# Forget-gate sums written by the matmul into all the partitions that the scores read, in place of eight transfers between partitions

## The reference, cut to what matters

```python
log_f = jax.nn.log_sigmoid(f_logit + b_forget)         # (B, 8 heads, 512)
c = jnp.cumsum(log_f, axis=-1)
logits = einsum('bhqd,bhkd->bhqk', q * Dh**-0.5, k)     # Dh = 64
logits = logits + c[:, :, q, None] - c[:, :, None, k]   # causal mask, softmax, @ v
```

## Time and profile before

| | us |
|---|---|
| median of 3 runs | 1793.53 |
| the runs | 1791.86, 1793.53, 1794.62 |
| the profiled execution | 1794.67 |
| its span | 1792.6 |
| mean granted TensorE clock | 0.996 |
| PE busy | 1767.9 (99% of the span) |
| PEld busy | 1491.5 (83%) |
| DVE busy | 1110.7 (62%) |
| ACT busy | 791.4 (44%) |
| POOL busy | 136.3 (8%) |

### The profile page before, as it was taken

How to read it: one execution, slowest core, us unless ns; L and a number is a source line. 1 busy time by engine, 2 the same in 40 slices (tenths; PEclk the granted TensorE clock), 3 DMA queues, 4 the chain that set the end, 5 groups by cost and what they waited for, 6 DMA issues and landing times.

```text
span 1792.6 us, 23145 instructions
## 1 busy us (share of the span) xinstructions
PE 1767.9 (99%) x8992; PEld 1491.5 (83%) x8992; DVE 1110.7 (62%) x1871; ACT 791.4 (44%) x1419; POOL 136.3 (8%) x133
## 2 busy tenths in 40 slices
PE   9999999999999999999999999999999999999998
PEld 7798788888888888887888888898888888888886
DVE  4578644344345666686764755656879776366375
ACT  6563432222235555544533433456766544144144
POOL 2003200000004100002000000023010110000000
PEclk9999999999999999999999999999999999999999
DMA  5212333333323222122333333322011233333331
GB/s 164 74 48 67 95 95 94 96 104 94 94 95 99 67 66 63 60 69 74 94 105 95 94 95 101 98 77 74 26 54 41 59 95 94 96 104 95 95 119 68
DMA packets 128328, 152.32 MB, mean 85 GB/s; under 512 B 9338, under 2 KB 102044, under 8 KB 128220
## 3 DMA queue, kind: packets, MB, share of 16 engines
q1 hardware_dynamic: 128060, 150.78, 27.4%
q10 hardware_dynamic: 160, 0.07, 0.0%
HBM read 148.59 MB, written 2.10 MB: 84 GB/s over the span
## 4 chain that ended last, share of the span: by engine, by line
PE 93%; DVE 3%; ACT 2%; issue 1%; POOL 1%; DMA 0%; SPq 0%; DVEq 0%; POOLq 0%; ACTq 0%
PE bk L1756 23%; PE bk L1758 22%; PE bk L1757 22%; PE bk L1785 5%; PE bk L1787 5%; PE bk L1786 5%; PE bk L1761 4%; PE bk L1857 2%; PE bk L1823 1%; PE bk L1830 1%; PE bk L1844 1%; DVE XT L1926 1%; PE bk L1846 1%; PE bk L1845 1%; ACT R L2105 0%
## 5 line engine op out<-in xcount | busy, mean ns | idle before, releaser
L1756 PE MATMUL bk<-R,WH 128*128 128x512 f32 x1764 | 691.8, 392 | 5.1 <-DVE R L1920 3.1
L1758 PE MATMUL bk<-R,WL 128*128 128x512 f32 x1764 | 687.4, 390 | 0.0
L1757 PE MATMUL bk<-R,WH 128*128 128x512 f32 x1764 | 687.1, 389 | 0.0
L1914 DVE TENSOR_TENSOR WL<-RAW,WH 128x1024 fp32r<-128x1024 f32 (+4 forms) x278 | 344.9, 1241 | 497.2 <-ACT WH L2101 496.5
L2101 ACT ACTIVATE WH<-RAW 128x1024 fp32r<-128x1024 f32 (+4 forms) x278 | 288.0, 1036 | 593.1 <-PE bk L1758 537.3
L1756 PEld LDWEIGHTS bk<-R,WH 128*128 128x128 f32 x1764 | 331.6, 188 | 73.3 <-issue 6.2
L1758 PEld LDWEIGHTS bk<-R,WL 128*128 128x128 f32 x1764 | 331.5, 188 | 69.6
L1757 PEld LDWEIGHTS bk<-R,WH 128*128 128x128 f32 x1764 | 331.8, 188 | 67.2
L1785 PE MATMUL bk<-WH,R 128*128 128x512 f32 (+4 forms) x528 | 187.4, 355 | 0.0
L1787 PE MATMUL bk<-WL,R 128*128 128x512 f32 (+4 forms) x528 | 179.1, 339 | 0.0
L1786 PE MATMUL bk<-WH,R 128*128 128x512 f32 (+4 forms) x528 | 178.7, 339 | 0.0
(11 more groups left out here) (155 smaller groups left out, 1617.6 us busy)
## 6 DMA issues: line engine op xcount, KB each, us to landing
RAW<-in_ffn_w_up_dram SPq DMA_DIRECT2D x176, 256.0 KB, 3.1
RAW<-in_ffn_w_down_dram SPq DMA_DIRECT2D x44, 512.0 KB, 3.7
RAW<-in_w_gate_dram SPq DMA_DIRECT2D x44, 256.0 KB, 2.8
RAW<-in_w_up_dram SPq DMA_DIRECT2D x44, 256.0 KB, 3.1
RAW<-in_w_down_dram SPq DMA_DIRECT2D x22, 512.0 KB, 3.7
RAW<-in_da_w_qkv_dram SPq DMA_DIRECT2D x32, 256.0 KB, 3.0
RAW<-in_w_out_dram SPq DMA_DIRECT2D x8, 512.0 KB, 3.7
RAW<-in_da_w_qkv_dram SPq DMA_DIRECT2D x8, 512.0 KB, 3.5
```

What stands on the lines that cost most here:

```text
L1756: e.matmul(dst, lh, rh, start=start, stop=False)
L1757: e.matmul(dst, lh, rl, start=False, stop=False)
L1758: return e.matmul(dst, ll, rh, start=False, stop=stop)
L1914: e.tensor_tensor(low, RAW[:, r, 0:m], high.bitcast(F32), ALU.subtract).then_inc(on["wlo_dve"], 1)
```

## The change

`gate_log` now writes the gates' logs not as 8 columns per token tile but as 128: in a slot of `FS` that POOL has zeroed (`gate_zero`), each head's value is repeated 4 times, and the 32 columns again in the second half, so that `gate_sum` has a 128-column stationary operand and writes c to partitions 0 to 31 and 64 to 95, four per head, with zeros in the others. The 8 DMAs, `gate_base` and `gate_cq` are gone. A new step `gate_rows` on DVE, once for the query's and once for the key's operand, is a `tensor_scalar` and a `scalar_tensor_tensor` over 128x512: high x column + (low x column + column), with three columns of 0, 1 and -1 each, so that of a head's four partitions one carries the high part, one the low part, and two a constant. It writes `R[cq]` and `ckf` directly. The planner's costs are changed with it.

```diff
-    "gate_in": {"dve": 2}, "gate_exp": {"act": 2}, "gate_log": {"dve": 1}, "gate_sum": {"pe": 1},
-    "gate_base": {"dve": 1}, "gate_rows": {}, "gate_cq": {"act": 1},
+    "gate_in": {"dve": 2}, "gate_exp": {"act": 2}, "gate_log": {"dve": 2}, "gate_zero": {"pool": 1}, "gate_sum": {"pe": 1},
+    "gate_rows": {"dve": 2},
...
-                "gate_in": 400.0, "gate_log": 190.0, ...
+                "gate_in": 400.0, "gate_log": 560.0, "gate_rows": 1450.0, ...
...
-            st = yield step("gate_log", dst=lf, z=z, e1=e1, after=[st.act])
+            st = yield step("gate_log", dst=FS[:, lx.i, 0:S], z=z, e1=e1, after=[st.act, zero.pool])
...
-            cut = yield from split_pair(c, BK[b.i][0:8, :], [st.pe], rows=slice(0, 8))
+            cut = yield from split_pair(c, BK[b.i][:, :], [st.pe])
...
-            for n, (d, s) in enumerate(((cqf, FG.cqf), (ckf, FG.ckf))):
-                st = yield step("gate_base", dst=d, c=C_BASE + n, after=counts([s.free, x_done[0]]))
-                bases.append(st.dve)
-            emit("gate_rows", rows=[(0, c.h.i, FG.cqf.i), (1, c.l.i, FG.cqf.i), (2, c.h.i, FG.ckf.i), (3, c.l.i, FG.ckf.i)],
-                 after=[cut, *bases])
-            placed = (s_c, 16 + 128)
-            ready_at[id(s_c), 144] = at_time(bases[1]) + 4000.0
...
-            st = yield step("gate_cq", dst=R[:, cq.i, :], src=cqf, after=counts([placed, cq.free]))
-            cq.ready = [st.act]
+            st = yield step("gate_rows", c=C_GATE, t=t, h=R[:, c.h.i, :], l=R[:, c.l.i, :], dst=R[:, cq.i, :],
+                            after=counts([cut, st.pe, cq.free]))
+            cq.ready = [st.dve]
+            st = yield step("gate_rows", c=C_GATE + 3, t=ckf, h=R[:, c.h.i, :], l=R[:, c.l.i, :], dst=ckf, after=counts(FG.ckf.free))
+            placed = st.dve
...
-                        mm = e.matmul(BK[st.bank][0:8, n * P:S], st.lf[:, 8 * n:8 * n + 8], st.tri[:, 0:S - n * P],
+                        mm = e.matmul(BK[st.bank][:, n * P:S], st.lf[:, n * P:n * P + P], st.tri[:, 0:S - n * P],
                                       start=n == 0, stop=n == 3)
...
+                    high, low, other = (CN[:, st.c + n:st.c + n + 1] for n in range(3))
+                    e.tensor_scalar(st.t, st.l.bitcast(F32), low, other, ALU.mult, ALU.add).then_inc(on["gate_rows_dve"], 1)
+                    w.wait_ge(on["gate_rows_dve"], st.dve0 + 1)
+                    times_add(st.dst, st.h.bitcast(F32), high, st.t, ALU.mult, ALU.add).then_inc(on["gate_rows_dve"], 1)
```

More of the change, by code:

```diff
@@ L193, in takes @@
                 "root_out": 760.0, "both_in": 370.0, "both_out": 370.0, "eighth": 170.0, "lam_in": 500.0, "lam": 500.0,
-                "gate_in": 400.0, "gate_log": 190.0, "out_in": 160.0, "z_sq": 160.0, "kv_mean": 170.0, "q_root": 170.0, "fg_cols": 160.0}.get(kind, 690.0)
+                "gate_in": 400.0, "gate_log": 560.0, "gate_rows": 1450.0, "out_in": 160.0, "z_sq": 160.0, "kv_mean": 170.0, "q_root": 170.0, "fg_cols": 160.0}.get(kind, 690.0)
     if kind == "rope":
@@ L1222, in gates @@
                 yield None
-            z, e1, lf = (small(32) for _ in range(3))
+            lx = yield from fslot()
+            zero = yield step("gate_zero", dst=FS[:, lx.i, 0:S], after=counts(lx.free))
+            z, e1 = (small(32) for _ in range(2))
             st = yield step("gate_in", z=z, e1=e1, flog=A0.flog, bf=bf, after=[*A0.tflog, (s_c, 16)])
             st = yield step("gate_exp", e1=e1, after=[st.dve])
-            st = yield step("gate_log", dst=lf, z=z, e1=e1, after=[st.act])
+            st = yield step("gate_log", dst=FS[:, lx.i, 0:S], z=z, e1=e1, after=[st.act, zero.pool])
@@ L1227, in gates @@
             b = yield from bank()
-            st = yield step("gate_sum", bank=b.i, lf=lf, tri=FS[:, tri.i, 0:S], after=counts([b.free, st.dve, (s_tri, 16)]))
+            st = yield step("gate_sum", bank=b.i, lf=FS[:, lx.i, 0:S], tri=FS[:, tri.i, 0:S], after=counts([b.free, st.dve, (s_tri, 16)]))
             fsl.put(tri, st.pe)
             c = yield from fill(Pair())
-            cut = yield from split_pair(c, BK[b.i][0:8, :], [st.pe], rows=slice(0, 8))
+            cut = yield from split_pair(c, BK[b.i][:, :], [st.pe])
@@ L1241, in gates @@
-            placed = (s_c, 16 + 128)
-            ready_at[id(s_c), 144] = at_time(bases[1]) + 4000.0
-            drop(c, placed)
-            while not tiles.fr:
-                yield None
-            cq = FG.cq = tiles.get()
-            st = yield step("gate_cq", dst=R[:, cq.i, :], src=cqf, after=counts([placed, cq.free]))
-            cq.ready = [st.act]
-            fsl.put(FG.cqf, st.act)
+            while not (flags.consts and tiles.fr):
+                yield None
+            cq, FG.ckf = tiles.get(), (yield from fslot())
@@ L2012, in vector_program @@
                         w.wait_ge(*done)
-                    times_add(st.dst, st.z, 0.0, st.e1, ALU.min, ALU.subtract).then_inc(on["gate_log_dve"], 1)
-                elif k == "gate_base":
+                    z4, e4 = (x.rearrange("p (t h) -> p t h", h=8).unsqueeze(3).to_broadcast([P, 4, 8, 4]) for x in (st.z, st.e1))
+                    halves = st.dst.rearrange("p (t s h x) -> p t s h x", t=4, s=2, h=16)
+                    for half in (0, 1):
+                        times_add(halves[:, :, half, 0:8, :], z4, 0.0, e4, ALU.min, ALU.subtract).then_inc(on["gate_log_dve"], 1)
+                elif k == "gate_rows":
                     for done in st.after:
                         w.wait_ge(*done)
-                    e.tensor_scalar(st.dst, XT[:, 0, :], 0.0, CN[:, st.c:st.c + 1], ALU.mult, ALU.add).then_inc(on["gate_base_dve"], 1)
+                    high, low, other = (CN[:, st.c + n:st.c + n + 1] for n in range(3))
+                    e.tensor_scalar(st.t, st.l.bitcast(F32), low, other, ALU.mult, ALU.add).then_inc(on["gate_rows_dve"], 1)
+                    w.wait_ge(on["gate_rows_dve"], st.dve0 + 1)
+                    times_add(st.dst, st.h.bitcast(F32), high, st.t, ALU.mult, ALU.add).then_inc(on["gate_rows_dve"], 1)
                 elif k == "scaled":
@@ L2253, in gpsimd_program @@
                     e.memset(st.dst, 0.0).then_inc(on["u_zero_pool"], 1)
+                elif k == "gate_zero":
+                    for done in st.after:
+                        w.wait_ge(*done)
+                    e.memset(st.dst, 0.0).then_inc(on["gate_zero_pool"], 1)
                 elif k == "window":
@@ L2296, in shape_constants @@
         c[:, C_SEL + h] = (p % 64 // 4 == 2 * h + p // 64)
-    c[:, C_BASE] = np.where((p % 64 < 32) & (p % 4 >= 2), -1.0, 0.0)
-    c[:, C_BASE + 1] = np.where((p % 64 < 32) & (p % 4 < 2), 1.0, 0.0)
+    for n, (x, v) in enumerate((((0,), 1.0), ((1,), 1.0), ((2, 3), -1.0), ((2,), 1.0), ((3,), 1.0), ((0, 1), 1.0))):
+        c[:, C_GATE + n] = np.where((p % 64 < 32) & np.isin(p % 4, x), v, 0.0)
     for rot, oc, os_ in ((16, C_CDA, C_SDA), (32, C_CML, C_SML)):
```

25 lines of the change are left out of this document (7 added, 18 removed).

## The result

The changed kernel takes **1822.85 us** in the median of 4 runs (1821.76 to 1824.33), against 1794.07 us for the kernel before on the same chip (4 runs, 1791.86 to 1795.12). The ratio is 1.0162 (95% interval 1.015 to 1.0175): 1.6% slower, 29 us, where 1790.7 us was forecast. The profiled execution has a span of 1822.1 us.

The account below looks back on a forecast made before the run. PE, busy 99% of the span, was taken as the bound, with gains only through holes and clock: 1.86 us plus 1.7 us in two of three runs, 3.0, less 0.2 for small holes, 1793.53 - 2.8 = 1790.7 us; range 1789.0 to 1793.6.

Parts of the forecast that it names:

- The rival on the slower side: Attention, 75 to 150 us: the new order has holes and dips, up to 4.6 us slower, 1798.1 us; chance 0.10.
- The hole of 1.86 us: PE's wait for ACT's `key_row` before the first `pair`, near 67 to 69 us, closes: 1.86 us gained in every run.
- each step behind 150 us lies 3.5 us earlier: Sign expected in the profile after: all steps past 150 us come 3.5 us earlier than in the profile before.
- The dip of 1.7 us, twice in three: PE's lowered clock right behind the hole, 69 to 75 us, goes with it: 1.7 us in two runs of three.
- `gate_log`, `gate_sum`, the splits: Gate steps widened to 128 columns or partitions: cost nothing; 0.8 us of `gate_sum` weight loads kept for the range.
- `gate_rows`: DVE ahead of `key_row`: 0.47 and 0.75 us per operand, operands ready 0.6 us before PE reaches `pair`.
- The rule of the skill against it: Two-SBUF-source operation in `gate_rows` at half throughput: 1.24 us estimated, `pair` 1.0 us later, a 0.4 us hole; not used in the sum.
- the DVE way is late as well: Slow `gate_rows` makes PE wait before `pair`: gain only 0 to 1.5 us, 1792.0 to 1793.5 us; chance 0.16.
- taken back at the next wait: PE's wait for DVE at 179 us grows, at most 3.5 us come back, time 1793.5 us; chance 0.10.

Follow-up runs that it names:

- experiment 7: The changed kernel with 60 columns more behind the constants, so R less WH is a multiple of 256 bytes again: 1792.24 us, ratio 0.9993.
- experiment 9: The changed kernel with R, KT and PT allocated directly behind the split weights and the constants behind them, no pad: 1791.15 us, ratio 0.9988.
- the control: The kernel before with 64 columns more behind the constants, putting R 256 bytes further on: 1793.65 us, ratio 1.0002.
- experiment 10: The kernel before with a pad of 32 bytes between R and KT, moving KT and PT but not R: 1794.12 us, ratio 1.001.
- experiment 1: The kernel before with its constants' tensor four columns wider, moving everything behind it by 32 bytes as after the change: 1826.08 us, ratio 1.0183.
- experiment 4: The kernel before with a pad of 32 bytes between FS and R, so the constants, TOK and FS stay: 1824.35 us, ratio 1.0169.
- experiment 6: The kernel before with a pad of 32 bytes in front of the split weights, moving weights and R alike: 1796.01 us, ratio 1.0007.
- experiment 8: The same run as the control: the kernel before with 64 columns more behind the constants, 1793.65 us, ratio 1.0002.
- the earlier trace: The profile of the kernel before from which the prediction was made, with the dip behind the hole: 1794.67 us, against a median of 1793.53 us.
- experiment 2: The changed kernel with eight columns more behind the constants, a shift of 64 bytes: 1799.78 us, ratio 1.0029.
- experiment 3: The changed kernel with 24 columns more behind the constants, a shift of 128 bytes: 1817.8 us, ratio 1.0133.
- experiment 5: TensorE alone, not the kernel: 128x512 float32r matmuls swept over places of both operands; 0.2269 us a matmul at difference 0, 0.2337 at 32 bytes.
- experiment 12: TensorE alone: the kernel's patterns of three at shifts of 0 to 224 bytes; R moving, 512 columns: 0.2265 us at 0, 0.2335 at 32.

## Why the prediction was wrong

**The step that failed** is one sentence ahead of all sums: "The change leaves the number of PE's matmuls and their moving columns alone, so it can act through holes and clock alone." Number and columns did stay, but the time of one did not: the 5292 matmuls of `gemm_f` take 31.6 us more from start to start, 0.7 us less waiting at 179 us included. All other starts together take 3.0 us less, with the closed hole and the dip behind it (1.86 + 1.7 us) among them; that is 28.6 us over PE's work, of the 29 us measured. The full diff had the cause (`C_END` 966 to 970) and the sum had no term for it; no rival had it either. The rival on the slower side expected holes between 75 and 150 us: there are none (PE 75.00 of 75 us busy). It had the right sign for a wrong reason.

The other steps, judged where the shift is 0 (experiments 7 and 9):

- *The hole of 1.86 us.* Right. PE's timeline has a row of 88x88 near 18 us and the `gemm_f` near 179 us that waits for DVE, the same steps in both orders. In the control, and then in the changed kernel of experiment 7:

```profile
18.07 0.49 PE L1761 MATMUL bk<-CN,FS 88*128 88x88 f32 x4 [0.48 <-issue]
...
179.67 0.47 PE L1756 MATMUL bk<-R,WH 128*128 128x512 f32 x1 [2.01 <-DVE R L1904]
```
```profile
18.71 0.49 PE L1751 MATMUL bk<-CN,FS 88*128 88x88 f32 x4 [0.47 <-issue]
...
178.81 0.47 PE L1746 MATMUL bk<-R,WH 128*128 128x512 f32 x1 [2.02 <-DVE R L1894]
```

  From the one to the other it is 161.60 us in the control and 160.10 us in the changed kernel; experiment 10 has 161.55 us, experiment 9 159.90 us. None of the four has a dip on the way (clock 1.00), so the change itself gives 1.5 to 1.7 us there, a little less than the hole. The profile before, with its dip, has 163.22 us there, so 3.1 us more than experiment 7, where "each step behind 150 us lies 3.5 us earlier" was forecast. In the changed kernel as measured it is 160.69 us: some of the gain is eaten by the slower matmuls on the way. Over whole runs, span times granted clock is 1783.8 and 1783.9 us in the mean of 11 runs each (experiments 7 and 9), against 1785.9 (27 runs) and 1785.5 us (21 runs) before: 2.1 and 1.6 us.
- *The dip of 1.7 us, twice in three.* Overpriced. Of the six profiles with the old order (the kernel before, experiments 1, 4, 6, 8 and 10) three have it behind this hole. The control, for one, reads a clock of 1.00 where the earlier trace rows had 0.72:

```profile
69.00:75.00 6.00, 6.00 (x54) 5.24 (x55) 4.63 (x18) 3.26 (x13) 0.00 (x0) 1.00 0.30 87
```

  And over runs nothing of it comes back: span times (1 - clock) is 5.9 and 6.1 us before, 6.5 and 5.9 us with the hole closed. The dips come behind other holes instead, and not always behind the same ones: the window around 580 us, which cost 1.8 us in the earlier trace rows, costs 0.17 x 20 = 3.4 us in experiment 7's profile (and in the control's), and nothing in experiment 9's:

```profile
570.00:590.00 20.00, 19.11 (x82) 15.79 (x82) 10.31 (x25) 5.24 (x11) 5.49 (x4) 0.83 0.23 75
```

  At other shifts the new order lost less to the clock, 3.3 and 3.2 us in experiments 2 and 3 against 6.8 us in the runs before beside them, so what a run loses by dips hangs on more than this hole. So the gain at a shift of 0 is near 2 us in place of 2.8, and within the range that was given, had the shift been 0: 1792.24 and 1791.15 us lie between 1789.0 and 1793.6.
- *`gate_log`, `gate_sum`, the splits.* Right in cost: the two operations end at 55.1 us in place of 54.6, but PE waits for nothing in front of `gate_sum`, and this profile lies some 0.7 us later from its start (the row of 88x88 is at 18.66 in place of 18.00 us). `gate_sum` to the next matmul is 57.94 - 55.87 = 2.07 us, no longer than the 2.25 us of the earlier trace rows, so its wider weight loads cost nothing. It is this measurement that shows it: the 1.7 us of the earlier trace rows are idle time of the weight loads, not of PE, and did not carry the argument. `lo` takes 0.69 us.
- *`gate_rows`.* Right for the large one, 0.75 us. The `tensor_scalar` took 0.55 in place of 0.47 us, and the margin in front of `pair` was 0.4 us rather than 0.6: the first `key_row` ends near 62.25 + 0.67 = 62.9 us and PE could begin 0.25 us later, at 63.2 us, while it arrives at 63.38 + 0.23 = 63.6 us. The 0.47 us were read from an operation on another source (XT); this one reads R. Whether that is the cause was not tested.
- *The rule of the skill against it.* The Trainium skill (Vector Engine (DVE) Microarchitecture Reference, section 7, "Points that are easy to get wrong") would have had the two-source operation at half the throughput. The trace has 0.75 us, as the row before; the rule didn't bite here.
- *Rival "the DVE way is late as well":* no wait in front of `pair`. *Rival "taken back at the next wait":* with the shift at 0 that wait is 2.0 us, as before, so nothing is taken back:

```profile
PE bk L1746 <- DVE R L1894: 2.0, 1, 2.0
```

The Trainium skill (SBUF — State Buffer, "Operand start alignment") asks of an operand only that it start at a multiple of its element size, and says that this "is about legality, not speed". All kernels here fulfil it, and their medians lie between 1791.15 and 1826.08 us; nothing in that rule would have warned.

## What to carry to other kernels

Where PE is busy for 99%, first compare the rate of its most frequent matmul between two kernels, in a window without holes: a count per 100 us shows 3% at a glance, and here the rate was worth 31.6 us where the hole was worth 1.9. A change that resizes a tensor moves every tensor behind it; allocate the operands of the hot matmuls first and side by side, at a distance that is a multiple of 256 bytes, and small tables behind them, so that no table can move them. This is shown for float32r operands of 128 stationary and 512 moving columns; narrower ones went by other places. When a small change brings a loss all over the program, put its allocation sizes alone into the old kernel: that one run tells places from instructions.

## What the runs showed of the hardware

- A 128x128 by 128x512 matmul in float32r at the full clock takes 0.2269 us from start to start when the moving operand stands a multiple of 256 bytes from the stationary one, 0.2294 us at 64 bytes past that, and 0.2325 to 0.2344 us at the other multiples of 32, with the other engines idle (experiment 5). In the kernels it is 0.2267 us at 0 and 0.2333 us at 32 bytes, and 100 us hold 443, 438, 432 and 430 of them at 0, 64, 128 and 32 bytes. The absolute place was seen to matter less (0.227 to 0.228 us at a difference of 0).
- With 256 columns most places lie within 0.003 us of each other in experiment 12, and 0 is among the slowest (0.1200 us; 0.123 in experiment 5).
- Fewer stationary columns (64, 32, 8) don't make a matmul of 512 moving columns faster than 0.228 to 0.232 us, but nearly take away the effect of the place (0.230 against 0.231 us at 0 and 32 bytes with 64 columns).
- Dips of the granted clock to 0.5, some 3.4 us long (one of 6.8 us near 580 us in the profiles of experiments 7 and 8), don't belong to one hole: at a shift of 0 the clock time lost over a run stayed near 6 us with one hole fewer.
